# State-space stage: the time steps' sums and rows, and the steps of groups 0 and 1, in later slots

## The chip, the core and the metric
The kernel runs on one core of one Trainium2 chip. The metric is the device time of one execution in microseconds; several executions of the same program give a median. TensorE (PE) multiplies matrices, VectorE (DVE) and ScalarE (ACT) work elementwise, GpSimd (POOL) computes the low parts of the weights, and SyncE (SP) issues the weight transfers.

## What is computed
Two blocks of a network run on 512 tokens of width 1024: a first block with a state-space branch, a dilated attention branch and a feed-forward part, then a second block of two layers with a gated delta rule and sparse attention. The change touches the state-space branch of the first block alone. What it computes, cut to its core:

```python
z, xbc, dt_raw, q, k, v, g_ssd, g_attn = jnp.split(rms_norm(x, norm1_g) @ w_in, IN_SPLITS, axis=-1)
xbc = silu(causal_dwconv(xbc, conv_w, conv_b))          # 8 groups of 4 heads: X (2 tiles), B, C
dt = softplus(dt_raw + dt_bias); A = -exp(a_log)
a_cs = cumsum(dt * A)                                   # per head, in chunks of 128 time steps
Ldec = exp(where(causal, a_cs[l] - a_cs[s], -inf))
y_diag = einsum(C, B, Ldec, X * dt)
states = einsum(B, exp(a_cs[-1] - a_cs), X * dt)        # carried from chunk to chunk
y_off = einsum(C, previous state, exp(a_cs))
y = (y_diag + y_off + d_skip * xs) * silu(z)
```

## The kernel before
All products run in fp32r with every operand split in a high and a low part. Weights come as a stream of units of 2048 columns (1 MB each): SyncE transfers a unit to `w_raw`, ScalarE writes its high part `w_hi` (L358, `split_unit`), GpSimd subtracts for the low part `w_lo` (L350, four instructions), and TensorE multiplies. A unit holds two half units. One half unit is one call of `gemm` (L369): 16 matmuls with `w_hi` (L379, L380), then 8 with `w_lo` (L385), all into one PSUM bank `g`. This is called a product below. The first product on a unit waits for its `w_hi`, and its last 8 matmuls for its `w_lo`.

The state-space stage goes through slots, numbered (g, n) with n from 0 to 3 and written out by `ssd_slots` (L756). Each slot has one product. In slots (0,0) to (7,3) its result is convolved over time and goes through a silu: for each, ScalarE taps the bank to `s_cv` (L889), VectorE adds three shifted taps (L962, `convolved`), ScalarE writes the silu to `s_xbc` (L904). Slot (g,n) is tile n of group g: 0 and 1 are X, 2 is B, 3 is C. TensorE has made the products of g = 0 before the loop. From slot (8,0) on the products are those of z.

Behind the product of each slot stand the steps of a group x, one each slot, with four slots for each group, from (x+1, 0) on:
- step 0, the turning (`turn`): TensorE transposes X and B (L784, L788) to `p` banks 0 to 2 and multiplies B with C into `p[3]` (L791, the score products); ScalarE copies B (L899); VectorE makes X times the time steps (L975) and masks the score products (L979);
- step 1, the decays (`decays`, L799): four matmuls spread rows of `s_rows` over the partitions, ScalarE takes their exponentials (`s_eb`, L916), VectorE makes two segments (L991, L994), ScalarE their exponentials (L878, heads 0 and 1);
- step 2, the states (`states`, L808): three matmuls, VectorE the other two segments, ScalarE their exponentials (heads 2 and 3), VectorE two scores (L998);
- step 3: VectorE the other two scores, and the recurrence of the states to `s_st` (L1003 to L1011);
- a slot later TensorE makes the group's output (L823, L825), which VectorE reads (L953).

Ahead of all groups stand the time steps. VectorE makes `s_a` in slot (0,1) (L702, with `s_pick` as its last write, L706). TensorE sums it in `pe_dt_sums` (L639, L640), VectorE copies the sums and makes the decay's argument (`dve_dt_decay`, L713 to L718), TensorE turns the copy in rows (`pe_dt_rows`, L727), ScalarE copies the rows (`act_dt_rows`, L734), VectorE corrects a part of them (`dve_dt_rows`, L740). All four stand before or in slot (1,0).

The order on each engine is written out by hand and every engine works strictly in its order; semaphores count up and waits are for the next count.

Of the kernel before, what the change touches and what calls it, by code (L numbers as in the profile page):

```python
# [20 lines left out]
P = 128  # L21
# [701 lines left out]
def pe_dt_rows(K, pe, pos):  # L723
    pe.wait_ge(K.sem("dt_a"), pos.next("dt_a"))
    pe.wait_ge(K.sem("g_free3"), pos.next("g_free3"))
    for c in range(NB):
        last = K.nc.tensor.matmul(K.g[3][:, c * P:c * P + P], K.s_acs4[:, c], K.mask("ident"),  # L727
                                  start=True, stop=True)
    last.then_inc(K.sem("turned"), 1)


def act_dt_rows(K, act, pos):
    act.wait_ge(K.sem("turned"), pos.next("turned"))
    act.activation(K.s_rows[:], K.g[3][:], ACT.Copy).then_inc(K.sem("exp_out"), 1)  # L734


def dve_dt_rows(K, dve, pos):
    dve.wait_ge(K.sem("exp_out"), pos.next("exp_out", 2))
    r = slice(32, 64)
    K.nc.vector.tensor_tensor(K.s_rows[r], K.g[3][r], K.s_rows[r].bitcast(F32), ALU.subtract).then_inc(pos.own, pos.tick())  # L740
    dve.wait_ge(pos.own, pos.ticks())
    dve.sem_inc(K.sem("g_free3"), 1)
# [13 lines left out]
def ssd_slots():  # L756

    slots, turn = [], 0
    for i in range(4 * GROUPS + 16):
        x, step = i // 4 - 1, i % 4  # L760
        core = (x, step) if 0 <= x < GROUPS else None
        out = x - 1 if step == 0 and 1 <= x <= GROUPS else None
        z = i - 4 * GROUPS if i >= 4 * GROUPS else None
        ring = {}
        for use, there in (("half", True), ("y", out is not None), ("sum", z is not None and z % 2 == 0 and z > 0)):
            if there and i == 3:
                ring[use] = 3
            elif there:
                ring[use] = turn % 3
                turn += 1  # L770
        slots.append((i // 4, step, z, core, out, ring))
    return slots


def pe_ssd(K, pe, pos):
# [3 lines left out]
    def turn(x):  # L779
# [9 lines left out]
        last.then_inc(K.sem("turned"), 1)  # L789
        for c in range(NB):  # L790
            last = t.matmul(K.p[3][:, c * P:c * P + P], xbc[:, 2, c * P:c * P + P], xbc[:, 3, c * P:c * P + P],  # L791
                            start=True, stop=True)
# [9 lines left out]
    def states(x):  # L802
        if x:
            pe.wait_ge(K.sem("y_read"), pos.next("y_read", 2))
        pe.wait_ge(K.sem("x2"), pos.next("x2"))
# [28 lines left out]
    for g, n, z, core, out, ring in ssd_slots():  # L834
# [4 lines left out]
        if (g, n) == (1, 0):  # L839
            pe_dt_sums(K, pe, pos)  # L840
            pe_dt_rows(K, pe, pos)
# [29 lines left out]
def act_ssd(K, act, pos):  # L871
# [10 lines left out]
    for g, n, z, core, out, ring in ssd_slots():  # L882
# [4 lines left out]
        b, step = ring["half"], None if core is None else core[1]  # L887
        if z is None:
            act.activation(K.s_cv[:, n % 2], K.g[b][:], ACT.Identity, scale=K.col("conv_w", g * 16 + n * 4 + 3),  # L889
                           bias=K.col("conv_b", g * 4 + n)).then_inc(K.sem("tap"), 1)  # L890
        else:
            if z == 0:
                act.wait_ge(K.sem("y_read"), pos.next("y_read", 14))
            act.activation(K.z_s[:, z % 2], K.g[b][:], ACT.Silu).then_inc(K.sem("z_s"), 1)
        if n % 2 and (g, n) != (0, 1):
            split_unit(K, act, pos, n // 2)
        if step == 0:
# [4 lines left out]
        if z is None:  # L902
            act.wait_ge(K.sem("conv"), pos.next("conv"))
            act.activation(K.s_xbc[:, g % 2, n], K.s_cv[:, n % 2], ACT.Silu).then_inc(K.sem("xbc"), 1)  # L904
# [15 lines left out]
        if (g, n) == (0, 3):  # L920
            act_dt_decay(K, act, pos)
            act_dt_rows(K, act, pos)
# [24 lines left out]
def dve_ssd(K, dve, pos):  # L947
# [71 lines left out]
    for g, n, z, core, out, ring in ssd_slots():  # L1019
# [5 lines left out]
        x, step = core if core is not None else (None, None)  # L1025
        if out is not None:
# [12 lines left out]
        else:  # L1039
# [3 lines left out]
            dve.sem_inc(K.sem(f"g_free{b}"), 1)  # L1043
        if step == 0:
# [4 lines left out]
        elif step == 2:  # L1049
            scores(0)  # L1050
            scores(1)
        if (g, n) == (0, 1):
            dve_dt(K, dve, pos)
        if (g, n) == (0, 3):
            dve_dt_decay(K, dve, pos)
            dve_dt_rows(K, dve, pos)
# [1906 lines left out]
```

## Time and profile before
| | |
|---|---|
| median of 3 runs | 3738.72 us (3729.16 to 3741.48) |
| profiled execution, its own time | 3724.99 us |
| its span | 3723.2 us, granted TensorE clock 0.986 of full |
| PE busy | 3611.1 us, 97% |
| DVE busy | 1820.8 us, 49% |
| ACT busy | 1410.3 us, 38% |
| POOL busy | 1406.1 us, 38% |

Times in the rows are microseconds from the start of the span. A row of the timeline has the start, the duration of the merged instructions, the engine, the line of the kernel, the operation, the tiles it writes and reads, their shapes, the count, and in square brackets the idle time of the engine ahead of it and what ended it.

### The profile page before, as it was taken

What the parts mean: (1) busy time and instruction counts of PE and PEld (TensorE: products, weight loads), DVE (VectorE), ACT (ScalarE), POOL (GpSimd) and SP (SyncE); (2) the same over time, 40 slices, a digit from 0 to 9 for tenths busy, and PEclk for the clock granted to TensorE, in tenths of its full rate; (3) what the DMA queues carried; (4) which work ended last, traced back from release to release, by engine and by line L of the source; (5) the groups of instructions that cost most, each with busy time, mean ns of one, the idle gap of its engine ahead of it and who ended that gap; (6) DMA issues with size and microseconds to landing.
All of it is one profiled execution on the core that took longest, in us unless ns stands there. A gap on an engine that the chain in (4) does not pass through costs nothing.

```text
span 3723.2 us, 48288 instructions
## 1 busy us (share of the span) xinstructions
PE 3611.1 (97%) x18696; PEld 2996.3 (80%) x18696; DVE 1820.8 (49%) x3291; ACT 1410.3 (38%) x2039; POOL 1406.1 (38%) x1092
## 2 busy tenths in 40 slices
PE   6999999999999999999999999999999999899998
PEld 5887888777788888888778988888888877888887
DVE  5887516654788664456475451113112467542111
ACT  5666424544322232223345442223222435543222
POOL 2333443223444444434311044445445421115444
PEclk9999999999999999999999999999999999999999
DMA  3121222111355655555310022223222310012222
GB/s 119 70 76 60 93 101 71 56 68 57 113 191 190 208 191 195 185 200 178 102 35 35 1 102 102 84 94 117 102 81 101 125 46 35 24 46 91 102 85 108
DMA packets 67325, 375.99 MB, mean 101 GB/s; under 512 B 7856, under 2 KB 8368, under 8 KB 39344
## 3 DMA queue, kind: packets, MB, share of 16 engines
q1 hardware_dynamic: 44192, 286.11, 21.5%
q10 hardware_dynamic: 22928, 86.99, 7.0%
q8 instruction: 147, 2.41, 0.3%
q14 instruction: 58, 0.48, 0.0%
HBM read 370.97 MB, written 2.10 MB: 100 GB/s over the span
## 4 chain that ended last, share of the span: by engine, by line
PE 57%; issue 24%; POOL 12%; DVE 4%; ACT 1%; POOLq 0%; DVEq 0%; ACTq 0%
PE g L379 13%; PE g L380 12%; PE g L385 12%; POOL w_lo L350 12%; PE g L364 3%; PE g L365 2%; PE g L366 2%; PE p L1899 1%; PE p L2075 1%; PE g L1878 1%; PE p L1889 1%; PE p L2081 1%; PE g L624 1%; PE g L620 1%; PE g L619 1%
## 5 line engine op out<-in xcount | busy, mean ns | idle before, releaser
L350 POOL TENSOR_TENSOR w_lo<-w_raw,w_hi 128x512 fp32r<-128x512 f32 (+1 forms) x1088 | 1405.9, 1324 | 2310.0 <-ACT w_hi L358 2310.0
L379 PE MATMUL g<-h_lo,w_hi 128*128 128x512 f32 x2400 | 949.3, 396 | 3.7 <-ACT w_hi L358 1.6
L380 PE MATMUL g<-h_hi,w_hi 128*128 128x512 f32 x2400 | 935.5, 390 | 0.0
L358 ACT ACTIVATE w_hi<-w_raw 128x2048 fp32r<-128x2048 f32 (+1 forms) x292 | 515.8, 1766 | 941.4 <-PE g L385 867.1
L385 PE MATMUL g<-h_hi,w_lo 128*128 128x512 f32 x2400 | 592.8, 389 | 1.2 <-POOL w_lo L350 1.2
L379 PEld LDWEIGHTS g<-h_lo,w_hi 128*128 128x128 f32 x2400 | 450.7, 188 | 106.4 <-issue 8.6
L380 PEld LDWEIGHTS g<-h_hi,w_hi 128*128 128x128 f32 x2400 | 450.7, 188 | 95.3 <-issue 3.1
L385 PEld LDWEIGHTS g<-h_hi,w_lo 128*128 128x128 f32 x2400 | 450.4, 188 | 95.1 <-POOL w_lo L350 1.6
L379 PE MATMUL g<-act_lo,w_hi 128*128 128x512 f32 x880 | 346.1, 393 | 0.0
L380 PE MATMUL g<-act_hi,w_hi 128*128 128x512 f32 x880 | 343.1, 390 | 0.0
L1650 DVE TENSOR_TENSOR p<-f_acc,g 128x512 f32<-128x512 f32 x84 | 58.5, 696 | 564.4 <-PE g L385 563.2
L1498 DVE SCALAR_TENSOR_TENSOR p<-ada_w,csilu,p 128x256 f32<-128x256 f32 x432 | 211.6, 490 | 52.4 <-DMA ada_w<-in_ada 29.6
L385 PE MATMUL g<-act_hi,w_lo 128*128 128x512 f32 x880 | 212.5, 389 | 0.0
L379 PEld LDWEIGHTS g<-act_lo,w_hi 128*128 128x128 f32 x880 | 165.3, 188 | 34.1
L385 PEld LDWEIGHTS g<-act_hi,w_lo 128*128 128x128 f32 x880 | 165.2, 188 | 34.3
L380 PEld LDWEIGHTS g<-act_hi,w_hi 128*128 128x128 f32 x880 | 165.3, 188 | 33.9
L364 PE MATMUL g<-h_hi,w_lo 128*128 128x512 f32 x416 | 179.5, 431 | 0.9 <-POOL w_lo L350 0.9
L1462 DVE SCALAR_TENSOR_TENSOR x<-g,mods,x 128x512 f32<-128x512 f32 x48 | 35.9, 749 | 277.9 <-PE g L385 267.3
L365 PE MATMUL g<-h_lo,w_hi 128*128 128x512 f32 x416 | 167.7, 403 | 0.0
L366 PE MATMUL g<-h_hi,w_hi 128*128 128x512 f32 x416 | 167.2, 402 | 0.0
L1580 ACT ACTIVATE f_acc<-g 128x512 f32<-128x512 f32 x84 | 50.2, 598 | 258.1 <-PE g L385 249.9
L1629 DVE TENSOR_TENSOR act_lo<-p,act_hi 128x512 fp32r<-128x512 f32 x110 | 76.1, 692 | 119.3 <-ACT act_hi L1561 108.1
(484 smaller groups left out, 5175.6 us busy)
## 6 DMA issues: line engine op xcount, KB each, us to landing
w_raw<-in_stream SPq DMA_DIRECT2D x212, 1024.0 KB, 4.8
ada_w<-in_ada ACTq DMA_DIRECT2D x144, 512.0 KB, 4.1
w_raw<-in_stream SPq DMA_DIRECT2D x80, 704.0 KB, 4.1
ada_w<-in_stream ACTq DMA_DIRECT2D x8, 512.0 KB, 4.4
n_w<-in_w ACTq DMA_DIRECT2D x4, 1024.0 KB, 10.1
x<-in_x SPq DMA_DIRECT2D x4, 512.0 KB, 9.7
b_w<-in_stream ACTq DMA_DIRECT2D x2, 1024.0 KB, 4.8
out_x<-x SPq DMA_DIRECT2D x4, 512.0 KB, 2.6
```

The source lines that it names most:

```text
L350: last = K.nc.gpsimd.tensor_tensor(K.w_lo[:, s, c], K.w_raw[:, s, c], K.w_hi[:, s, c].bitcast(F32), ALU.subtract)
L358: act.activation(K.w_hi[:, s, 0:width], K.w_raw[:, s, 0:width], ACT.Copy).then_inc(K.sem("w_hi"), 1)
L364: nc.tensor.matmul(out, w_lo, h_hi, start=start, stop=False)
L365: nc.tensor.matmul(out, w_hi, h_lo, start=False, stop=False)
L366: return nc.tensor.matmul(out, w_hi, h_hi, start=False, stop=stop)
L379: t.matmul(K.g[b][:], K.w_hi[:, s, w], lo[:, k, :], start=starts and i == 0, stop=False)
L380: t.matmul(K.g[b][:], K.w_hi[:, s, w], hi[:, k, :], start=False, stop=False)
L385: last = t.matmul(K.g[b][:], K.w_lo[:, s, w], hi[:, k, :], start=False, stop=ends and i == len(ks) - 1)
L1498: v.scalar_tensor_tensor(out, w[:, i * 256:i * 256 + 256], scalar(i), acc, ALU.mult, ALU.add).then_inc(pos.own, pos.tick())
L1580: act.activation(K.f_acc[:, s], K.g[2 * s][:], ACT.Silu).then_inc(K.sem("f_s"), 1)
L1629: v.tensor_tensor(K.act_lo[:, u], K.p[1 if conv else u % 2][:], K.act_hi[:, u].bitcast(F32), ALU.subtract).then_inc(K.sem("act_lo"), 1)
L1650: v.tensor_tensor(K.p[s][:], K.f_acc[:, s], K.g[2 * s + 1][:], ALU.mult).then_inc(K.sem("f_u"), 1)
```

## The change
- The sums of the time steps (`pe_dt_sums`) stand behind the product of slot (1,1), not (1,0); the rows (`pe_dt_rows`) behind that of (1,2), and they use the bank `p[3]` and not `g[3]`. The bank is handed on by a semaphore of its own, `dt_rows`, for which the score products of group 0 wait.
- VectorE's decay steps stand ahead of the convolution of slot (0,3), not behind it. `act_dt_rows` stands in slot (1,2) behind the tap, `dve_dt_rows` in slot (1,2) behind the convolution.
- Group 0 begins in slot (1,2) and not (1,0), group 1 in slot (2,1) and not (2,0). Both have three slots: VectorE makes all four scores and the recurrence in the slot of step 2. The outputs of groups 0 and 1 stand in slots (2,1) and (3,0); before, in (2,0) and (3,0). From group 2 on nothing is moved.
- Since group 0 still reads its half of `s_xbc` in slot (2,1), ScalarE writes the silus of (2,0) and (2,1) together there, after waiting for VectorE to have read the output, and waits ahead of the tap of (2,2) for the first of them.

```diff
--- before.py
+++ after.py
@@ -722,23 +722,23 @@

 def pe_dt_rows(K, pe, pos):
     pe.wait_ge(K.sem("dt_a"), pos.next("dt_a"))
-    pe.wait_ge(K.sem("g_free3"), pos.next("g_free3"))
     for c in range(NB):
-        last = K.nc.tensor.matmul(K.g[3][:, c * P:c * P + P], K.s_acs4[:, c], K.mask("ident"),
+        last = K.nc.tensor.matmul(K.p[3][:, c * P:c * P + P], K.s_acs4[:, c], K.mask("ident"),
                                   start=True, stop=True)
     last.then_inc(K.sem("turned"), 1)


 def act_dt_rows(K, act, pos):
     act.wait_ge(K.sem("turned"), pos.next("turned"))
-    act.activation(K.s_rows[:], K.g[3][:], ACT.Copy).then_inc(K.sem("exp_out"), 1)
+    act.activation(K.s_rows[:], K.p[3][:], ACT.Copy).then_inc(K.sem("exp_out"), 1)


 def dve_dt_rows(K, dve, pos):
     dve.wait_ge(K.sem("exp_out"), pos.next("exp_out", 2))
     r = slice(32, 64)
-    K.nc.vector.tensor_tensor(K.s_rows[r], K.g[3][r], K.s_rows[r].bitcast(F32), ALU.subtract).then_inc(pos.own, pos.tick())
-    dve.wait_ge(pos.own, pos.ticks())
+    K.nc.vector.tensor_tensor(K.s_rows[r], K.p[3][r], K.s_rows[r].bitcast(F32), ALU.subtract
+                              ).then_inc(K.sem("dt_rows"), 1)
+    dve.wait_ge(K.sem("dt_rows"), pos.next("dt_rows"))
     dve.sem_inc(K.sem("g_free3"), 1)


@@ -756,10 +756,12 @@
 def ssd_slots():

     slots, turn = [], 0
+    begins = [6, 9] + [4 * x + 4 for x in range(2, GROUPS)]
+    cores = {at + step: (x, step) for x, at in enumerate(begins) for step in range(4 if x > 1 else 3)}
+    outs = {9 if x == 0 else 4 * x + 8: x for x in range(GROUPS)}
     for i in range(4 * GROUPS + 16):
-        x, step = i // 4 - 1, i % 4
-        core = (x, step) if 0 <= x < GROUPS else None
-        out = x - 1 if step == 0 and 1 <= x <= GROUPS else None
+        step = i % 4
+        core, out = cores.get(i), outs.get(i)
         z = i - 4 * GROUPS if i >= 4 * GROUPS else None
         ring = {}
         for use, there in (("half", True), ("y", out is not None), ("sum", z is not None and z % 2 == 0 and z > 0)):
@@ -787,6 +789,8 @@
         for c in range(NB):
             last = t.transpose(K.p[2][:, c * P:c * P + P], xbc[:, 2, c * P:c * P + P], ident)
         last.then_inc(K.sem("turned"), 1)
+        if x == 0:
+            pe.wait_ge(K.sem("dt_rows"), pos.next("dt_rows"))
         for c in range(NB):
             last = t.matmul(K.p[3][:, c * P:c * P + P], xbc[:, 2, c * P:c * P + P], xbc[:, 3, c * P:c * P + P],
                             start=True, stop=True)
@@ -802,6 +806,8 @@
     def states(x):
         if x:
             pe.wait_ge(K.sem("y_read"), pos.next("y_read", 2))
+        else:
+            pe.wait_ge(K.sem("g_free3"), pos.next("g_free3"))
         pe.wait_ge(K.sem("x2"), pos.next("x2"))
         pe.wait_ge(K.sem("seg"), pos.next("seg"))
         for c in range(3):
@@ -836,8 +842,9 @@
         if g == 0:
             continue
         gemm(K, pos, s, (ring["half"],), K.h_hi, K.h_lo, c0=n % 2 * P, fresh=n % 2 == 0)
-        if (g, n) == (1, 0):
+        if (g, n) == (1, 1):
             pe_dt_sums(K, pe, pos)
+        if (g, n) == (1, 2):
             pe_dt_rows(K, pe, pos)
         if out is not None:
             output(out, ring["y"])
@@ -885,23 +892,30 @@
         else:
             act.wait_ge(K.sem("part"), pos.next("part"))
         b, step = ring["half"], None if core is None else core[1]
+        if (g, n) == (2, 2):
+            act.wait_ge(K.sem("xbc"), 9)
         if z is None:
             act.activation(K.s_cv[:, n % 2], K.g[b][:], ACT.Identity, scale=K.col("conv_w", g * 16 + n * 4 + 3),
                            bias=K.col("conv_b", g * 4 + n)).then_inc(K.sem("tap"), 1)
         else:
             if z == 0:
-                act.wait_ge(K.sem("y_read"), pos.next("y_read", 14))
+                act.wait_ge(K.sem("y_read"), pos.next("y_read", 12))
             act.activation(K.z_s[:, z % 2], K.g[b][:], ACT.Silu).then_inc(K.sem("z_s"), 1)
         if n % 2 and (g, n) != (0, 1):
             split_unit(K, act, pos, n // 2)
+        if (g, n) == (1, 2):
+            act_dt_rows(K, act, pos)
         if step == 0:
             act.wait_ge(K.sem("turned"), pos.next("turned"))
             act.activation(K.s_btok[:].rearrange("p c n -> p (c n)"), K.p[2][:], ACT.Copy).then_inc(K.sem("turned_out"), 1)
         if step == 2:
             exps(core[0], (2, 3))
         if z is None:
-            act.wait_ge(K.sem("conv"), pos.next("conv"))
-            act.activation(K.s_xbc[:, g % 2, n], K.s_cv[:, n % 2], ACT.Silu).then_inc(K.sem("xbc"), 1)
+            if (g, n) == (2, 1):
+                act.wait_ge(K.sem("y_read"), pos.next("y_read", 2))
+            for m in {(2, 0): (), (2, 1): (0, 1)}.get((g, n), (n,)):
+                act.wait_ge(K.sem("conv"), pos.next("conv"))
+                act.activation(K.s_xbc[:, g % 2, m], K.s_cv[:, m % 2], ACT.Silu).then_inc(K.sem("xbc"), 1)
         elif z % 2 == 0 and z:
             z_deviation(K, act, pos, K.g[ring["sum"]])
         elif z % 2:
@@ -919,7 +933,6 @@
             act_dt(K, act, pos)
         if (g, n) == (0, 3):
             act_dt_decay(K, act, pos)
-            act_dt_rows(K, act, pos)
     pos.skip("y_read", 2)


@@ -1023,6 +1036,8 @@
             pos.skip("part")
         b = ring["half"]
         x, step = core if core is not None else (None, None)
+        if (g, n) == (0, 3):
+            dve_dt_decay(K, dve, pos)
         if out is not None:
             output(out, ring["y"])
         if step == 1:
@@ -1041,6 +1056,8 @@
             v.tensor_tensor(K.y[:, z], K.y[:, z], K.z_s[:, z % 2], ALU.mult).then_inc(K.sem("z_y"), 1)
             dve.wait_ge(K.sem("z_y"), pos.next("z_y"))
             dve.sem_inc(K.sem(f"g_free{b}"), 1)
+        if (g, n) == (1, 2):
+            dve_dt_rows(K, dve, pos)
         if step == 0:
             inputs(x)
         elif step == 1:
@@ -1049,11 +1066,12 @@
         elif step == 2:
             scores(0)
             scores(1)
+            if x < 2:
+                scores(2)
+                scores(3)
+                states(x)
         if (g, n) == (0, 1):
             dve_dt(K, dve, pos)
-        if (g, n) == (0, 3):
-            dve_dt_decay(K, dve, pos)
-            dve_dt_rows(K, dve, pos)
         if z is not None and z > 1:
             if z % 2 == 0:
                 z_normal(K, dve, pos, z // 2 - 1, ring["sum"])
```

TensorE, slots (1,0) and (1,1), behind the 8 matmuls with `w_lo` that end the product of (1,0); L784 to L791 are the turning of group 0. Before:

```order
L385 MATMUL g<-h_hi,w_lo 128x512 x8
L639 MATMUL p<-s_a,masks 128x128
L640 MATMUL p<-s_a,masks 128x128
L727 MATMUL g<-masks,s_acs_93 128x128 x4
L784 MATMUL p<-masks,s_xbc 128x128 x8
L788 MATMUL p<-masks,s_xbc 128x128 x4
L791 MATMUL p<-s_xbc 128x128 x4
L379 MATMUL g<-h_lo,w_hi 128x512
```

With the change, behind the product of slot (1,2); the two sums alone stand one product earlier:

```order
L385 MATMUL g<-h_hi,w_lo 128x512 x8
L726 MATMUL p<-masks,s_acs_93 128x128 x4
L786 MATMUL p<-masks,s_xbc 128x128 x8
L790 MATMUL p<-masks,s_xbc 128x128 x4
L795 MATMUL p<-s_xbc 128x128 x4
L379 MATMUL g<-h_lo,w_hi 128x512
```

Rows and turning have moved two products back.

VectorE, group 0, from the last segment to the output (L953, with the change L966). Before:

```order
L994 TENSOR_TENSOR s_ce<-s_xbc,s_eb 128x512
L962 SCALAR_TENSOR_TENSOR s_cv<-g,cols,s_cv 128x511
L962 SCALAR_TENSOR_TENSOR s_cv<-g,cols,s_cv 128x510
L962 SCALAR_TENSOR_TENSOR s_cv<-g,cols,s_cv 128x509
L998 TENSOR_TENSOR s_m<-s_m,s_cbt 128x512 x4
L1003 COPY s_st<-g 128x256
L1007 TENSOR_TENSOR s_st<-s_st,s_eb 128x256
L1011 TENSOR_TENSOR s_st<-s_st,g 128x256
L1007 TENSOR_TENSOR s_st<-s_st,s_eb 128x256
L1011 TENSOR_TENSOR s_st<-s_st,p 128x256
L962 SCALAR_TENSOR_TENSOR s_cv<-g,cols,s_cv 128x511
```

With the change:

```order
L1007 TENSOR_TENSOR s_ce<-s_xbc,s_eb 128x512
L975 SCALAR_TENSOR_TENSOR s_cv<-g,cols,s_cv 128x511
L975 SCALAR_TENSOR_TENSOR s_cv<-g,cols,s_cv 128x510
L975 SCALAR_TENSOR_TENSOR s_cv<-g,cols,s_cv 128x509
L1011 TENSOR_TENSOR s_m<-s_m,s_cbt 128x512 x4
L1016 COPY s_st<-g 128x256
L1020 TENSOR_TENSOR s_st<-s_st,s_eb 128x256
L1024 TENSOR_TENSOR s_st<-s_st,g 128x256
L1020 TENSOR_TENSOR s_st<-s_st,s_eb 128x256
L1024 TENSOR_TENSOR s_st<-s_st,p 128x256
L966 SCALAR_TENSOR_TENSOR y<-s_xbc,cols,g 128x512 x2
```

Up to the last step of the states the list is the same; behind it the convolution (three instructions) that stood ahead of the output is gone.

ScalarE, group 1, from the exponentials of its decays (L916) to the silu's table load: in the second piece a weight unit (L358) stands between the tap and the second half of the exponentials. Before:

```order
L916 ACTIVATE s_eb<-p 128x512 x4
L878 ACTIVATE s_m<-s_m,s_nacs 128x128 x8
L889 ACTIVATE s_cv<-g,cols 128x512
L878 ACTIVATE s_m<-s_m,s_nacs 128x128 x8
L904 ACT_TABLE_LOAD
```

With the change:

```order
L930 ACTIVATE s_eb<-p 128x512 x4
L885 ACTIVATE s_m<-s_m,s_nacs 128x128 x8
L898 ACTIVATE s_cv<-g,cols 128x512
L358 ACTIVATE w_hi<-w_raw 128x2048
L885 ACTIVATE s_m<-s_m,s_nacs 128x128 x8
L918 ACT_TABLE_LOAD
```

The split has moved ahead of the exponentials of heads 2 and 3.

## Rows read from the trace of the kernel before
**Rows 1.** The page, part 1: busy time, share of the span, instructions.
```profile
PE 3611.1 (97%) x18696; PEld 2996.3 (80%) x18696; DVE 1820.8 (49%) x3291; ACT 1410.3 (38%) x2039; POOL 1406.1 (38%) x1092
```
**Rows 2.** Timeline of PE, 60 to 140 us: start, duration, what.
```profile
67.34 0.77 PE L639 MATMUL p<-s_a,masks 128*128 128x128 f32 x2 [4.97 <-DVE s_pick L706]
...
74.83 2.08 PE L727 MATMUL g<-masks,s_acs 128*128 128x128 f32 x8 [6.30 <-DVE s_acs L718]
...
78.80 1.06 PE L791 MATMUL p<-s_xbc 128*128 128x128 f32 x8
...
79.61 0.47 PE L379 MATMUL g<-h_lo,w_hi 128*128 128x512 f32 x1
...
85.18 1.09 PE L799 MATMUL p<-s_rows,s_pick 128*128 128x512 f32 x4
...
104.54 0.68 PE L823 MATMUL g<-s_m,s_X 128*64 128x128 f32 x8
...
107.77 1.09 PE L784 MATMUL p<-masks,s_xbc 128*128 128x128 f32 x8
...
115.51 1.07 PE L799 MATMUL p<-s_rows,s_pick 128*128 128x512 f32 x4
...
134.87 0.68 PE L823 MATMUL g<-s_m,s_X 128*64 128x128 f32 x8
```
**Rows 3.** Stretches, PE alone: us, length, busy, granted clock, DMA share, GB/s.
```profile
64.00:66.00 2.00, 0.00 (x0) 0.66 0.00 0
...
78.00:80.00 2.00, 2.00 (x17) 0.92 0.57 143
```
**Rows 4.** Timeline of DVE, 67 to 105 us.
```profile
67.11 2.31 DVE L962 SCALAR_TENSOR_TENSOR s_cv<-g,cols,s_cv 128x511 f32<-128x511 f32 x3
...
73.25 0.29 DVE L713 COPY s_acs<-p 128x128 f32<-128x128 f32 x1
...
74.10 0.68 DVE L718 COPY s_acs<-p 128x512 f32<-128x512 f32 x1
...
77.58 0.68 DVE L740 TENSOR_TENSOR s_rows<-g,s_rows 32x512 fp32r<-32x512 f32 x1 [2.80 <-ACT s_rows L734]
...
91.12 0.69 DVE L991 TENSOR_TENSOR s_m<-p,s_acs 128x512 f32<-128x512 f32 x1 [2.61 <-ACT s_eb L916]
...
98.87 2.50 DVE L998 TENSOR_TENSOR s_m<-s_m,s_cbt 128x512 f32<-128x512 f32 x4
...
102.66 1.28 DVE L1007 TENSOR_TENSOR s_st<-s_st,s_eb 128x256 f32<-128x256 f32 x1
...
103.97 0.42 DVE L1011 TENSOR_TENSOR s_st<-s_st,p 128x256 f32<-128x256 f32 x1
```
**Rows 5.** Timeline of ACT, 69 to 76 us.
```profile
69.99 0.76 ACT L889 ACTIVATE s_cv<-g,cols 128x512 f32<-128x512 f32 x1
70.65 1.90 ACT L358 ACTIVATE w_hi<-w_raw 128x2048 fp32r<-128x2048 f32 x1
73.14 0.63 ACT L904 ACTIVATE s_xbc<-s_cv 128x512 f32<-128x512 f32 x1 [0.58 <-DVE s_cv L962]
73.78 1.28 ACT L663 ACT_TABLE_LOAD   x1
75.08 0.31 ACT L663 ACTIVATE s_dec<-s_dec 128x128 f32<-128x128 f32 x1
```
**Rows 6.** Timeline of POOL, 72 to 78 us.
```profile
72.63 4.95 POOL L350 TENSOR_TENSOR w_lo<-w_raw,w_hi 128x512 fp32r<-128x512 f32 x4 [18.93 <-ACT w_hi L358]
```
**Rows 7.** Timeline of PE, DVE and POOL late in the stage, 318 to 332 us.
```profile
326.72 1.15 PE L823 MATMUL g<-s_m,s_X 128*64 128x128 f32 x8 [8.73 <-DVE s_st L1011]
...
331.98 1.98 PE L856 MATMUL g<-z_q,masks 128*128 128x512 f32 x4
...
320.39 3.41 DVE L998 TENSOR_TENSOR s_m<-s_m,s_cbt 128x512 f32<-128x512 f32 x2
...
318.31 6.62 POOL L350 TENSOR_TENSOR w_lo<-w_raw,w_hi 128x512 fp32r<-128x512 f32 x4 [12.63 <-ACT w_hi L358]
```

## Prediction
> **What bounds the kernel now.** I read the page first: TensorE is busy for 97% of the span [rows 1], so this change, which moves work inside one stage, can only matter where TensorE stands still there or will come to do so. The next view is the timeline of TensorE around the first state-space groups. It stands still twice: 4.97 us before the sums of the time steps and 6.30 us before their rows [rows 2]. Behind the first pause the granted clock falls from 2.4 to 1.2 GHz (0.66 in 64 to 66 us, a mixture of the two levels) and is whole again only within 78 to 80 us (0.92) [rows 3], so the work between the pauses and just behind them runs at half speed. That is the prize: 11.3 us of idle time and about 2 us of slow clock.
>
> The third view is the same timeline further on, since the change also squeezes groups 0 and 1. From the first matmul of a group's decays to the first of its output, TensorE takes 85.18 to 104.54 us for group 0, and 115.51 to 134.87 us for group 1: 19.36 us both times [rows 2]. In that stretch it runs three products (a product is the 24 matmuls of one half unit, 79.61 to 85.18, 5.57 us [rows 2]) and the states. The fourth view, VectorE and ScalarE over the same 19.36 us, says who sets that length: VectorE's last step of the states starts at 103.97 and takes 0.42, and the output starts 0.15 us behind it [rows 2, 4]. So TensorE now has exactly enough products to cover the other two engines, and none to spare.
>
> **Part 1, sums and rows of the time steps.** The product of slot (1,1) now stands in the 4.97 us pause. It starts at 62.4 (67.34 less 4.97 [rows 2]) and ends near 68.0, and the sums follow at once, since what they need has come at 67.34. The 6.30 us pause is filled only partly. The product of slot (1,2) is the first on another weight unit, whose high part ScalarE splits from 70.65 for 1.90 us [rows 5], so it can't start before 72.6. TensorE pauses from about 68.5 to 72.6. Its low part is ready when GpSimd ends, 72.63 + 4.95 = 77.6 [rows 6], so this product ends near 79.4; the rows and the first turning then end by 81.4 (from 74.83 to 78.80 they take 4.0 at the low clock [rows 2], so about 2.0 at the high one). Nothing is lost by any of this yet.
>
> The score products of group 0 are the first that wait for `dt_rows`. In VectorE's queue that step now stands behind the convolution of slot (1,2), and this ends a ladder in which the two engines take turns. VectorE has convolved slot (0,2) at 67.11 + 2.31 = 69.4 [rows 4]. The decay steps follow, 1.5 us (from 73.25 to 0.68 past 74.10 [rows 4]), to 71.0; the convolution of (0,3), 2.31, to 73.3; ScalarE's silu 0.63, table load 1.28 and exponential 0.31 [rows 5], to 75.6. Each slot now costs 0.76 + 2.31 + 0.63 = 3.7 us [rows 4, 5]: two slots bring 83.0, the first tap and the convolution of (1,2) 86.1, and the row step 0.68 [rows 4] 86.8. TensorE had reached this point by 81.4, so it waits about 5 us: a new stall in place of the old one. Before, the row step stood ahead of that ladder, at 77.58 [rows 4].
>
> From there: score products 0.81 (78.80 to 79.61), the product of (1,3) 5.57 [rows 2], and about 2.0 for a clock that falls in a pause of this size. For that 2.0 the nearest row is the stall of 8.73 us late in the stage: the output behind it takes 326.72 to 331.98, 5.26 us, against 104.54 to 107.77, 3.23 us [rows 2, 7]. The decays of group 0 start at 86.8 + 0.8 + 5.6 + 2.0 = 95.2, where before they started at 85.18. They then have two products more behind them, so against the old order TensorE is 85.18 + 2 x 5.57 - 95.2 = 1.1 us ahead: of the 13.4 us hardly anything is left.
>
> **Part 2, three slots for each of the first two groups.** Decays, states and output of group 0 now stand in slots (1,3), (2,0) and (2,1): two products between decays and output, not three. VectorE's work in between is the same list (four segments, one convolution, four scores, the states), because the second convolution was behind the states before and is behind them now. Nothing in that list but its head waits for TensorE. So the output starts 19.36 us after the decays, and TensorE, with one product less to do, stands still for 5.57 us. This comes once in each group.
>
> Group 0: output at 95.2 + 19.4 = 114.6. From there the output, the turning of group 1 and a product take 104.54 to 115.51, 10.97 us [rows 2], plus 2.0 for the clock: decays of group 1 at 127.5.
>
> Group 1: its second exponentials now fall into slot (2,3), in which ScalarE first splits a weight unit (1.90 [rows 5]); before, that slot of the group had no split. The exponentials still come in time, but GpSimd's four subtractions now run beside VectorE's scores. With GpSimd beside them two scores took 3.41 us [rows 7], where four took 2.50 [rows 4], so 2.2 more for two. I take 2.2 for the four; 0 if GpSimd comes late, 4.3 if all four are caught. The trace shows it also at 102.66, where a step of the states takes 1.28 [rows 4]. The Trainium skill, page "SBUF — State Buffer", section "Who interferes with whom", says that a VectorE instruction with two inputs in SBUF and a GpSimd instruction that reads SBUF exclude each other for a whole instruction. The scores are of that kind and the trace agrees (1.7 us for one of 0.62); by the rule alone the cost would be at most four GpSimd instructions, near my upper end.
>
> Output of group 1: 127.5 + 19.4 + 2.2 = 149.1, and 2.0 for the clock: 151.1. From that point both orders have the same work behind and ahead of them; before, it was reached at 134.87 [rows 2].
>
> **Sum: +16.3 us**, call it 16. In it: -1.1 up to the decays of group 0, two stalls of 5.6, two low clocks of 2.0, and GpSimd 2.2. Against the profiled execution (span 3723.2, its time 3725.0) this makes 3741. That execution is faster than two of the three runs shown; on their median, 3738.7, it makes **3755 us** (+0.43%). The bounds: if the clock never falls in the three new stalls, 6 us less; if GpSimd meets nothing, 2.2 less; so +8. With all four scores caught and another step of the states in each group (1.28 for about 0.4), +20. Later stages follow TensorE and are only shifted: the weight transfers are issued as GpSimd frees a unit, which follows the products. The deferred silus of slot (2,0) are hidden: ScalarE has the whole product of (2,2) for them.
>
> **The rivals.**
> *A small loss.* Same stalls, but the clock keeps its level and GpSimd's work lands between VectorE's steps: +8 to +11, 3747 to 3750. For it: a stall of 5 us is shorter than the one of 8.7 I took the price from. Against it: the clock fell in the pause of 4.97 us already [rows 2, 3].
> *The stalls don't come, not slower.* One mechanism: the distance from decays to output is elastic, and shrinks to the 13.8 us of TensorE's own work (19.36 - 5.57). Then output 1 starts at 86.8 + 0.8 + 5.6 + 13.8 + 11.0 + 13.8 = 131.8, 3 us early, 3736; if the row step comes without a wait too, some 8 us early, 3730; and if the product of (1,2) finds its unit ready the whole 13.4 is gained, 3725. It decides at a distance of 15.3 us, where the output would start at 134.87. For it: VectorE idles 2.6 us ahead of the first segment, waiting for ScalarE [rows 4]. Against it: both groups show the same 19.36, and behind that first segment VectorE works without a pause to the end of the states.
> *A larger loss.* The stalls repeat in group 2, or the clock stays low through a whole product: over +20, above 3759. Against it: group 2 has its four slots again.
>
> **How the numbers follow.** The smallest change that a measurement of this kernel tells from none is about 0.3%, 11.2 us. The forecast, between +11.2 and +20, has 0.60 and lies wholly on the slower side; a small loss 0.22, within 0.3%; the elastic distance 0.13, of which 0.08 faster by over 0.3% and 0.05 within it; a larger loss 0.05. That gives faster 0.08, same 0.27, slower 0.65. The range leaves out the elastic distance and most of the larger loss, takes in +8 on a run a few microseconds below the median and +20 with as much above: 3740 to 3763.
>
> **What would show it.** In the new profile: the waits for `s_pick` and for the decay copy are gone from TensorE; its score products wait some 5 us for VectorE's row step; the output of groups 0 and 1 waits some 5.5 us and up to 8 us for the last step of the states; decays to output is again about 19.4 us for group 0, and 20 to 22 for group 1; the granted clock shows three low spells between 82 and 155 us; output 1 starts near 149. The prediction is wrong if the output waits stay under 2 us, if the row step ends before 82 us, or if the start of output 1 lies before 140.

## The result and the profile after

| | before | with the change |
|---|---|---|
| median | 3729.19 us (13 runs, 3723.83 to 3741.48) | 3744.76 us (13 runs, 3738.76 to 3755.09) |
| ratio | | 1.0041, 95% interval 1.0029 to 1.0052 |
| profiled execution, span | 3723.2 us | 3751.6 us |
| mean granted clock | 0.986 | 0.982 |
| PE busy | 3611.1 us | 3626.5 us |

The change makes the kernel 15.6 us slower, 0.41%, with an interval of 0.29 to 0.52%. The profiled execution of the changed kernel (3753.4 us by its own time) is one of its slower ones, so the spans differ by 28.4 us, more than the medians do. Where the change itself stands in the trace is read from the first and last start of two groups of matmuls behind the stage: first the products on the finished state-space output (`y_hi`), then those on the activations of the feed-forward parts. Before:

```profile
L380 PE MATMUL g<-y_hi,w_hi x128: 389/389/389, 448.2 to 531.1; 128*128 128x512 f32 x128
...
L380 PE MATMUL g<-act_hi,w_hi x880: 389/389/397, 1229.8 to 3705.1; 128*128 128x512 f32 x176
```

With the change:

```profile
L380 PE MATMUL g<-y_hi,w_hi x128: 389/389/389, 464.2 to 547.1; 128*128 128x512 f32 x128
...
L380 PE MATMUL g<-act_hi,w_hi x880: 387/389/398, 1246.0 to 3734.3; 128*128 128x512 f32 x176
```

At 448 us the delay is 16.0, at 1230 it is 16.2: nothing is given back and nothing added over these stages. The 12 us more by the end of this one execution (28.4 less 16.2) arise behind 1246 us, where no instruction has moved; they are not in the medians.

TensorE's waits between 50 and 160 us, with the change:

```profile
PE g L829 <- DVE s_st L1024: 13.9, 2, 7.6
PE g L379 <- ACT w_hi L358: 4.3, 1, 4.3
PE p L795 <- DVE s_rows L739: 3.6, 1, 3.6
```

Both old pauses (4.97 and 6.30 us [rows 2]) are gone; in their place stand four: for the weight unit, for the row step, and for the last step of the states ahead of each of the first two outputs. The timeline of TensorE, answering to [rows 2] (L803 are the decays, L829 the output, L786 the turning of the next group):

```profile
72.38 0.79 PE L379 MATMUL g<-h_lo,w_hi 128*128 128x512 f32 x1 [4.34 <-ACT w_hi L358]
...
80.48 1.05 PE L726 MATMUL p<-masks,s_acs 128*128 128x128 f32 x8
...
86.47 1.16 PE L795 MATMUL p<-s_xbc 128*128 128x128 f32 x8 [3.63 <-DVE s_rows L739]
...
92.96 1.09 PE L803 MATMUL p<-s_rows,s_pick 128*128 128x512 f32 x4
...
113.00 1.15 PE L829 MATMUL g<-s_m,s_X 128*64 128x128 f32 x8 [6.24 <-DVE s_st L1024]
...
119.00 1.10 PE L786 MATMUL p<-masks,s_xbc 128*128 128x128 f32 x8
...
126.75 1.07 PE L803 MATMUL p<-s_rows,s_pick 128*128 128x512 f32 x4
...
148.15 1.15 PE L829 MATMUL g<-s_m,s_X 128*64 128x128 f32 x8 [7.61 <-DVE s_st L1024]
...
161.41 1.09 PE L803 MATMUL p<-s_rows,s_pick 128*128 128x512 f32 x4
```

Read it in the steps of the sum. Decays to output (92.96 to 113.00, 126.75 to 148.15) is 20.04 us in group 0 and 21.40 in group 1, where it was 19.36 in both. The output itself takes 6.0 us (113.00 to 119.00) and not 3.23, since it starts at the low clock. The decays of group 2 start at 161.41. In the kernel before they start at 145.85, one period of 30.34 us behind those of group 1 [rows 2]:

```profile
145.85 1.09 PE L799 MATMUL p<-s_rows,s_pick 128*128 128x512 f32 x4
```

The difference is 15.6 us, which is that of the medians.

VectorE over the same time:

```profile
85.73 0.68 DVE L739 TENSOR_TENSOR s_rows<-p,s_rows 32x512 fp32r<-32x512 f32 x1
...
106.64 2.50 DVE L1011 TENSOR_TENSOR s_m<-s_m,s_cbt 128x512 f32<-128x512 f32 x4
...
109.51 1.48 DVE L1020 TENSOR_TENSOR s_st<-s_st,s_eb 128x256 f32<-128x256 f32 x1
...
139.95 5.89 DVE L1011 TENSOR_TENSOR s_m<-s_m,s_cbt 128x512 f32<-128x512 f32 x4
```

and GpSimd beside the last of these rows:

```profile
138.99 6.30 POOL L350 TENSOR_TENSOR w_lo<-w_raw,w_hi 128x512 fp32r<-128x512 f32 x4 [24.24 <-ACT w_hi L358]
```

The row step ends at 86.4. The four scores of group 1 take 5.89 us instead of 2.50 [rows 4], with GpSimd's four subtractions beside them, which themselves take 6.30 instead of 4.95 [rows 6].

The granted clock (us, length, PE busy, clock, DMA share, GB/s):

```profile
70.00:72.00 2.00, 0.00 (x0) 0.74 0.00 0
...
76.00:78.00 2.00, 2.00 (x7) 0.56 0.00 0
...
84.00:86.00 2.00, 0.00 (x0) 1.00 0.00 0
...
112.00:114.00 2.00, 1.00 (x10) 0.50 0.03 8
...
146.00:148.00 2.00, 0.00 (x0) 0.50 0.68 197
```

There are three low spells. Each begins in a pause of TensorE (of 4.34, 6.24 and 7.61 us) and reaches into the work behind it. In the pause of 3.63 us, in which TensorE stands from 82.8 to 86.5, the clock stays at 2.4 GHz.

### The profile page after: what moved, and what is told of

Same layout as the page of the kernel before. It is cut to its first block, busy times and chain, and to the rows that moved or that the text cites. A ratio compares the mean times of both kernels' runs of the same rounds, so it can differ in the third digit from the quotient of the medians.

```text
span 3751.6 us, 48289 instructions
## 1 busy us (share of the span) xinstructions
PE 3626.5 (97%) x18696; PEld 3008.2 (80%) x18696; DVE 1823.9 (49%) x3291; ACT 1409.5 (38%) x2039; POOL 1405.6 (37%) x1092
## 4 chain that ended last, share of the span: by engine, by line
PE 47%; issue 31%; POOL 16%; DVE 5%; ACT 1%; POOLq 0%; DVEq 0%; ACTq 0%
POOL w_lo L350 16%; PE g L379 9%; PE g L380 9%; PE g L385 9%; PE g L364 2%; PE g L366 2%; PE g L365 2%; PE p L1917 2%; PE p L2093 1%; PE g L1896 1%; PE p L1907 1%; PE p L2099 1%; PE p L1929 1%; PE g L620 0%; PE g L624 0%
## 5 line engine op out<-in xcount | busy, mean ns | idle before, releaser
L358 ACT ACTIVATE w_hi<-w_raw 128x2048 fp32r<-128x2048 f32 (+1 forms) x292 | 515.6, 1766 | 937.6 <-PE g L385 863.3
```

What stands on the lines that cost most here:

```text
L358: act.activation(K.w_hi[:, s, 0:width], K.w_raw[:, s, 0:width], ACT.Copy).then_inc(K.sem("w_hi"), 1)
```

## The experiments

The landmark is the start of the decays of group 2, behind which all these kernels but the last have the same work left. It is measured from the start of the write of `s_pick`, which does not depend on the edits: 78.8 us in the kernel before, 94.6 with the change. Landmarks and distances are each read from the one profiled execution of a kernel, and a fall of the clock that comes in one execution and not in another moves them by some 1.6 us, as `split_behind` shows. `split_behind`, `rows_early` and `conv_behind` were executed only once, so they have no median to compare.

### The stalls with TensorE kept at work

```diff
     def output(x, b):
-        pe.wait_ge(K.sem("mce"), pos.next("mce", 4))
+        if x < 2:
+            pe.wait_ge(K.sem("mce"), pos.next("mce", 1))
+            for i in range((16, 24)[x]):
+                t.matmul(K.p[3][:], K.mask_r[:, 0], K.h_hi[:, i % 8], start=True, stop=True)
+        pe.wait_ge(K.sem("mce"), pos.next("mce", 3 if x < 2 else 4))
```

> The changed kernel, with TensorE given idle work in the two stalls ahead of the outputs of groups 0 and 1: once the first score of the group is made, 16 and 24 matmuls whose result nobody reads. Theory (the stalls are set by VectorE and ScalarE, and the low clock behind them is a cost of its own): output 0 still starts near 113 us and output 1 at 21.4 us behind its decays, but the granted clock stays at full, so output 0 to the decays of group 1 takes 11.0 us and not 13.75, and the decays of group 2 start some 5 us earlier than 161.4, at 156 to 157. Rival (the clock costs nothing, since the other engines set the pace there as well): the decays of group 2 start at 161 as in the changed kernel.

Measured: the matmuls nobody reads, and the output behind them.

```profile
107.55 3.93 PE L823 MATMUL p<-h_hi,mask_r 128*128 128x512 f32 x16 [0.65 <-DVE s_m L1015]
...
113.18 0.68 PE L833 MATMUL g<-s_m,s_X 128*64 128x128 f32 x8 [1.70 <-DVE s_st L1028]
...
116.41 1.09 PE L786 MATMUL p<-masks,s_xbc 128*128 128x128 f32 x8
...
124.14 1.07 PE L803 MATMUL p<-s_rows,s_pick 128*128 128x512 f32 x4
...
145.63 0.68 PE L833 MATMUL g<-s_m,s_X 128*64 128x128 f32 x8 [1.59 <-DVE s_st L1028]
```

Output 0 starts when it did, 20.05 us behind its decays, though TensorE now works almost up to it: the other engines set that distance. The output takes 3.23 us again, and output 0 to the decays of group 1 takes 10.96 and not 13.75. The landmark is at 89.6, 5.0 us earlier; the ratio to the kernel before is 1.0029 (1.0015 to 1.0044). So of the 15.6 us, 5.0 are the clock behind the two stalls.

### The split behind the exponentials

```diff
-        if n % 2 and (g, n) != (0, 1):
+        if n % 2 and (g, n) not in ((0, 1), (2, 3)):
             split_unit(K, act, pos, n // 2)
...
         if step == 2:
             exps(core[0], (2, 3))
+        if (g, n) == (2, 3):
+            split_unit(K, act, pos, n // 2)
```

> The changed kernel, with ScalarE splitting the weight unit of slot (2,3) behind the second exponentials of group 1 and not ahead of them. Theory (GpSimd's four subtractions beside VectorE's scores made the four scores take 5.89 us and not 2.50): the scores take about 2.5 us, one or two steps of the states may take up to 1.3 us more each instead, and decays to output of group 1 is 19.4 to 21 us, not 21.40. The decays of group 2 start 1 to 2 us earlier than 161.4. Rival (the scores are slow for want of the exponentials): they stay at 5 to 6 us.

```profile
140.52 3.56 DVE L1013 TENSOR_TENSOR s_m<-s_m,s_cbt 128x512 f32<-128x512 f32 x4
...
144.46 1.03 DVE L1022 TENSOR_TENSOR s_st<-s_st,s_eb 128x256 f32<-128x256 f32 x1
...
145.98 0.92 DVE L1022 TENSOR_TENSOR s_st<-s_st,s_eb 128x256 f32<-128x256 f32 x1
```

The scores take 3.56 us, not 5.89 (expected were 2.5), though their exponentials now come earlier, not later: the rival falls. GpSimd begins at 141.90, 1.4 us into the scores, and the part of them that is slow follows it. 2.3 us are won there, and two steps of the states lose 1.1 together (1.03 and 0.92 for 0.43 each). Decays to output of group 1 is 20.17 us instead of 21.40. The landmark gains only 0.3 us, at 94.3: in this execution the clock fell in the pause ahead of the score products, and the product of slot (1,3) took longer (decays of group 0 at 27.8 from `s_pick`, not 26.2), which took back 1.6. By that distance the edit is worth 1.2 us; that the landmark gained less than the 1 to 2 us expected is the clock's doing.

### The rows behind the sums

```diff
         if (g, n) == (1, 1):
             pe_dt_sums(K, pe, pos)
-        if (g, n) == (1, 2):
             pe_dt_rows(K, pe, pos)
...
-        if (g, n) == (1, 2):
-            act_dt_rows(K, act, pos)
...
             act_dt_decay(K, act, pos)
+            act_dt_rows(K, act, pos)
...
-        if (g, n) == (1, 2):
+        if (g, n) == (1, 0):
             dve_dt_rows(K, dve, pos)
```

> The changed kernel, with the rows of the time steps right behind the sums in slot (1,1), ScalarE's copy at the end of slot (0,3) and VectorE's row step behind the convolution of slot (1,0). Theory (the score products of group 0 wait 3.63 us for a row step that stands behind a ladder of convolutions): this wait is gone, the rows fit in the pause ahead of the product of slot (1,2), and the decays of group 0 start some 3.5 us earlier, near 89.5 and not 92.96; everything behind moves with them, output 1 to near 144.5. Rival (the distance from decays to output is elastic and takes up the gain): output 1 stays at 148.

```profile
71.69 1.16 PE L726 MATMUL p<-masks,s_acs 128*128 128x128 f32 x8 [2.71 <-DVE s_acs L718]
73.32 0.80 PE L379 MATMUL g<-h_lo,w_hi 128*128 128x512 f32 x1 [0.48 <-ACT w_hi L358]
...
89.10 1.19 PE L803 MATMUL p<-s_rows,s_pick 128*128 128x512 f32 x4 [0.82 <-DVE s_cbt L990]
...
107.84 1.15 PE L829 MATMUL g<-s_m,s_X 128*64 128x128 f32 x8 [4.84 <-DVE s_st L1022]
...
141.57 1.15 PE L829 MATMUL g<-s_m,s_X 128*64 128x128 f32 x8 [7.59 <-DVE s_st L1022]
```

The wait for the row step is gone, and the rows fit in the pause for the weight unit. The decays of group 0 start 21.4 us behind `s_pick` (89.10 less 67.73) instead of 26.2: 4.8 us. 3.6 of them are the wait, less 0.8 for a new one for VectorE's inputs; 0.9 come since the rows' matmuls stand in the pause, and 1.0 since the product of (1,2) is done sooner (the turning starts 12.7 us behind `s_pick`, against 80.48 less 66.78, 13.7, for the rows ahead of it). The landmark is at 86.4, 8.3 us earlier. The other 3.5 are not that wait. 1.3 of them lie in the distance to output 0, which is 18.7 and not 20.0, as GpSimd's subtractions now meet fewer of VectorE's steps (the first of the states takes 0.42 us and not 1.48). 2.1 lie behind the two outputs, where the low clock costs 1.4 and 1.6 us and not 2.8 and 2.3. Whether a second execution would give these 3.5 again is not shown. The elastic rival falls: the gain grows on its way, it is not taken up.

### One group with three slots in the kernel before

```diff
-        out = x - 1 if step == 0 and 1 <= x <= GROUPS else None
+        out = 0 if i == 7 else x - 1 if step == 0 and 2 <= x <= GROUPS else None
...
-        elif step == 3:
+        elif step == 3 and x:
             scores(2)
             scores(3)
             states(x)
...
             scores(0)
             scores(1)
+            if x == 0:
+                scores(2)
+                scores(3)
+                states(x)
```

> The kernel before with one edit: group 0 has three slots, its scores and states in slot (1,2) and its output in slot (1,3), one slot earlier. Theory (decays to output takes 19.4 us whatever TensorE has to do): output 0 still starts at 104.5 us, now with one product less behind it, so TensorE stands still for about 5.5 us ahead of it and runs slowly for some 2 us behind it; the decays of group 2, 145.8 before, come 7 to 8.5 us later. Rival (the distance is elastic and shrinks to TensorE's own 13.9 us): output 0 starts near 99, and nothing behind moves by more than 1 us.

```profile
86.27 1.09 PE L799 MATMUL p<-s_rows,s_pick 128*128 128x512 f32 x4
...
105.59 1.15 PE L823 MATMUL g<-s_m,s_X 128*64 128x128 f32 x8 [5.53 <-DVE s_st L1011]
...
154.87 1.09 PE L799 MATMUL p<-s_rows,s_pick 128*128 128x512 f32 x4
```

This is the cleanest test, as nothing of the time steps is moved. Decays to output takes 19.32 us, as ever, and TensorE stands still for 5.53 us: the length of one product. The landmark is 87.2, 8.4 us later than before: 5.6 for the product, 2.4 for the slow clock behind the stall (18.95 us from output 0 to the decays of group 1, less 10.97 and one product), and 0.4 that arose ahead of the decays of group 0 (18.6 us from `s_pick`, not 18.2). The ratio is 1.0021 (1.0007 to 1.0036), some 8 us: half of what the whole change costs comes with one group that has lost a slot.

### The convolutions behind the states

```diff
         if z is None:
-            convolved(g, n, b)
+            if (g, n) not in ((2, 0), (2, 3)):
+                convolved(g, n, b)
...
                 states(x)
+            if (g, n) in ((2, 0), (2, 3)):
+                convolved(g, n, b)
```

> The changed kernel, with VectorE's convolutions of slots (2,0) and (2,3) behind the states of groups 0 and 1 and no longer ahead of their scores. Theory (behind its first segment VectorE's list sets the distance from decays to output): decays to output falls by one convolution, 2.3 to 2.5 us, in each of the two groups: from 20.04 to about 17.7 and from 21.40 to about 19; the decays of group 2 start 4 to 5 us earlier than 161.4. Rival (something else than VectorE's list sets it, ScalarE's exponentials or TensorE's states): the distances change by less than 1 us.

The decays and outputs of groups 0 and 1:

```profile
94.28 1.09 PE L803 MATMUL p<-s_rows,s_pick 128*128 128x512 f32 x4
...
110.30 0.68 PE L829 MATMUL g<-s_m,s_X 128*64 128x128 f32 x8 [2.24 <-DVE s_st L1024]
...
122.92 1.07 PE L803 MATMUL p<-s_rows,s_pick 128*128 128x512 f32 x4
...
142.09 1.15 PE L829 MATMUL g<-s_m,s_X 128*64 128x128 f32 x8 [5.39 <-DVE s_st L1024]
```

The distances fall to 16.02 and 19.17, by 4.0 and 2.2 us. The theory said one convolution each, 2.3. Group 0 gains 1.6 more because its states now end before GpSimd begins: both their steps take 0.43 us, not 1.48 and 0.92. In group 1 the 2.2 agree only by luck. VectorE, two of its four scores:

```profile
136.28 0.73 DVE L1011 TENSOR_TENSOR s_m<-s_m,s_cbt 128x512 f32<-128x512 f32 x1 [1.32 <-ACT s_m L885]
137.45 1.23 DVE L1011 TENSOR_TENSOR s_m<-s_m,s_cbt 128x512 f32<-128x512 f32 x1 [0.44 <-ACT s_m L885]
```

VectorE now waits 1.8 us for ScalarE's second exponentials, which stand behind the weight split there, so in this group the rival holds for a part. This loss was made up, as the scores, which now begin ahead of GpSimd, themselves take 3.3 us and not 5.89, against 1.1 more for the states. The landmark is at 88.2, 6.4 us earlier; the clock behind the outputs gave 1.8 of it, and took 1.6 ahead of the decays of group 0.

### Three edits together

> The changed kernel with three edits together: rows behind the sums, the two convolutions behind the states, the split of slot (2,3) behind the exponentials. Theory (three causes in a row on one chain, so their costs add): from the start of s_pick to the decays of group 2, 94.6 us in the changed kernel and 78.8 before, it takes 94.6 - 8.3 - 4.7 - 1 = 81 us (by the runs of the first two edits 8.3 and about 1, by estimate 4.7), still 1 to 3 us more than before; the time is within 0.15% of before. Rival (the causes cover each other): 84 us or more.

This is the changed kernel with the rows behind the sums, the convolutions behind the states, and the split behind the exponentials, by the three diffs above. The landmark is at 80.4, expected 81; the ratio to the kernel before is 1.0000 (0.9987 to 1.0013). The waits ahead of the two outputs are 1.96 and 2.94 us. The causes lie on one chain and their costs nearly add: the single gains were 8.3, 6.4 and 0.3 us, together 15.0, and the three edits together win 14.2. Mended, the change is worth nothing: two groups still have a slot too few, and these two waits with the low clock behind them (1.7 and 2.9 us) make 9.5 us. The first of them:

```profile
104.02 0.68 PE L829 MATMUL g<-s_m,s_X 128*64 128x128 f32 x8 [1.96 <-DVE s_st L1024]
```

and the clock behind it:

```profile
104.00:106.00 2.00, 1.98 (x30) 0.81 0.04 8
```

### TensorE one product ahead, all groups with four slots

The core of the edit to the kernel before, on TensorE; beside it the bank `p[3]` with the semaphore `dt_rows` as in the change, ScalarE's copy of the rows behind the split of slot (0,3), and VectorE's decay steps ahead of the convolution of (0,3) with the row step behind it.

```diff
-        if (g, n) == (1, 0):
+        if (g, n) == (1, 1):
             pe_dt_sums(K, pe, pos)
             pe_dt_rows(K, pe, pos)
...
+        if g == 1:
+            core = (0, n - 1) if n else None
         if core is not None and core[1] < 3:
             (turn, decays, states)[core[1]](core[0])
```

> The kernel before, every group with its four slots and its output where it was. TensorE makes the product of slot (1,1) ahead of the sums, rows and turning of group 0, and that of (1,2) ahead of its decays; VectorE makes its decay steps ahead of the convolution of (0,3), ScalarE copies the rows right behind the split. Theory (the idle time before the rows can be filled if nothing is put behind the ladder and no group loses a slot): the row step ends near 74 us, the turning near 76, and ScalarE and VectorE, which now set the pace, bring output 0 near 98.5 to 101 and not 104.5, after a stall of TensorE of 2 to 5 us; the decays of group 2 start 3 to 6 us earlier than 145.8, and the time is 3 to 6 us lower, 0.1 to 0.15%. Rival (each product moved forward is paid for again by a stall of its own length): the decays of group 2 at 145 to 147, the time as before.

The row step on VectorE:

```profile
73.03 0.68 DVE L739 TENSOR_TENSOR s_rows<-p,s_rows 32x512 fp32r<-32x512 f32 x1 [0.57 <-ACT s_rows L733]
```

and TensorE:

```profile
82.90 1.09 PE L801 MATMUL p<-s_rows,s_pick 128*128 128x512 f32 x4
...
98.43 0.68 PE L827 MATMUL g<-s_m,s_X 128*64 128x128 f32 x8 [2.23 <-DVE s_st L1018]
```

and the clock behind its start:

```profile
98.00:100.00 2.00, 1.57 (x29) 1.00 0.00 0
```

Of the 11.3 us of pauses 5.4 stay gone: the landmark is at 73.4 against 78.8, within what was expected. The ratio is 0.9990 (0.9978 to 1.0001), a median 3.8 us lower but not clear of no change by itself. Decays to output of group 0 is 15.5 us here and not 19.4. So the 19.36 us are no fixed time of the other engines behind the decays. Before, ScalarE's tap of slot (1,1), which with a convolution and a silu stands ahead of the exponentials, waits for the product that ends as the decays start. Here that product was done one product earlier, and the exponentials start 2.8 us behind the decays instead of 5.3. In the three-slot groups of the changed kernel the decays again follow directly on the product that the tap waits for, and the exponentials start 5.3 us behind them.

### The same for the late stall

```diff
             scores(2)
             scores(3)
             states(x)
+            if z == 3:
+                z_normal(K, dve, pos, 0, z_bank)
...
-            if z % 2 == 0:
+            if z == 2:
+                z_bank = ring["sum"]
+            elif z % 2 == 0:
                 z_normal(K, dve, pos, z // 2 - 1, ring["sum"])
```

> The kernel of turn_one_later with one more edit of the same kind, late in the stage: VectorE makes the last two scores and the states of group 7 ahead of the normalisation of the first two z tiles, not behind it. Theory (output 7 waits 8.7 us only because the list on VectorE ahead of the states holds 5.8 us of normalisation, with 3.75 us of waiting for ScalarE ahead of it, and the clock falls behind that wait): the wait ahead of output 7 falls to under 2 us, the output takes 3.2 and not 5.3 us; if the normalisation becomes late for nobody, the stage is 8 to 10 us shorter than that of turn_one_later, 13 to 15 us shorter than before, and the time 0.3 to 0.4% below before. Rival (the stall moves: the normalisation's bank and the squares behind it come late and TensorE waits there for as long): under 3 us gained over turn_one_later.

TensorE's waits, 60 to 400 us:

```profile
PE g L379 <- DVEq L1054: 2.7, 1, 2.7
...
PE g L862 <- DVEq L1054: 2.4, 1, 2.4
PE g L827 <- DVE s_st L1018: 2.4, 2, 2.3
```

The wait of 8.7 us ahead of output 7 [rows 7] is gone, the output takes 3 us again, but two waits of 2.4 and 2.7 us on VectorE's next steps have come behind it, so theory and rival each hold for a part. Behind the second of them the matmuls take 0.63 us instead of 0.39, so the clock has fallen there too. The products on `y_hi` start at 438.2 us; in `turn_one_later` at 442.7, before at 448.2. That is 4.5 us gained over `turn_one_later`, where 8 to 10 were expected. The ratio to the kernel before is 0.9979 (0.9967 to 0.9992): this version is faster than the kernel before by 0.2%, which is clear of no change but less than the 0.3 to 0.4% expected.

## Why the prediction was right

The forecast was slower, by 16 us; measured are 15.6. The mechanism held. That the sum of 16.3 came within 0.7 us is luck in part, since its terms missed by up to 2.2 us and in both directions. The absolute figure, 3755, is 10 us too high, since the median of three runs that it was put on, 3738.7, lies above the 3729.2 of thirteen.

*The time steps.* The row step was to end at 86.8 us and ended at 86.4: the ladder of taps, convolutions and silus was read correctly, and `rows_early` shows that it is the cause. TensorE came to it at 82.8 and not 81.4, since the clock fell already in the pause for the weight unit (0.74 in 70 to 72 us), which I had not counted. It cost nothing there, as TensorE had to wait for VectorE anyway. The wait was 3.6 us, not 5.

*The clock behind that wait.* Here a term was wrong: I took 2.0 us for a fall in a pause of 3.6 to 5 us and it did not come, so the decays of group 0 started at 92.96 and not 95.2. In two of the other runs, `split_behind` and `conv_behind`, it did come, after the same pause, and cost 1.6 us. So of the three low spells that were to show between 82 and 155 us there are two; the third of the profile lies earlier, behind the pause for the weight unit.

*The three-slot groups.* The forecast was one product, 5.57 us, of stall in each. `old_three_slots` shows it alone: 5.53 us and an unchanged 19.3 from decays to output. In the changed kernel the stalls are 6.24 and 7.61, because VectorE's list is longer by what GpSimd adds: 0.7 us in group 0, for which I had only a place in the upper bound, and 2.0 in group 1, where the forecast was 2.2. The four scores alone lost 3.4, near my upper end of 4.3; the steps of the states behind them, slow in the other groups, were free again and gave 0.9 of it back, and 0.5 came back ahead of them, where one instruction had taken 1.17 us and now took 0.68. The rule of the Trainium skill (page "SBUF — State Buffer", section "Who interferes with whom") fits: four instructions of 1.24 us could have cost 5.0 at most, and `split_behind` moves the loss with GpSimd.

*The clock behind the stalls.* Forecast 2.0 each; measured, from each output to the next decays, 2.8 behind output 0 (13.75 less 10.97) and 2.3 behind output 1 (13.26 less 10.97). `stall_filled` gives both back, 5.0 us.

*The rivals.* The elastic distance, in a group that gives up a slot, is refuted by `old_three_slots` and by `rows_early`. The 15.5 us of `turn_one_later` are another case, as there one more product stands between the product that the tap waits for and the decays. The small loss and the larger one did not come. The errors went both ways: 2.2 less at the first clock term, 1.1 more at the later two, 0.5 more for GpSimd.

## What to carry to other kernels

When steps of a pipeline are moved to fill a pause, compare each distance between two of TensorE's steps with the time that the other engines need in between. Where the one exactly covers the other, as with the 19.36 us here, each product taken out of it comes back as a stall of its own length, and in the changed kernel the clock added nearly half as much again. Look also at where the other engines' chain begins: it began here at the end of a product and not at the decays, and having that product done earlier shortened the distance to 15.5 us. Moving the filling work ahead of the waiting step, and the waited-for step ahead of its ladder, won 5 us in the trace where moving the steps back lost 16. An engine's order matters at both ends: what is put behind a ladder waits for all of it.

## What the runs showed of the hardware

The low clock behind the waits of 5.5, 6.2 and 7.6 us in `old_three_slots` and in the changed kernel cost 2.4, 2.8 and 2.3 us more, and in `stall_filled`, where TensorE had work in the pause, it did not come, though nobody reads the result. The length of the pause by itself decides neither whether the clock falls nor what that costs:

- Ahead of the score products of group 0 the clock stayed up behind 3.47 and 3.63 us and fell behind 3.68 and 3.75.
- Ahead of output 0 it fell behind 1.96 us in `three_mended` and 2.24 in `conv_behind`, at a cost of 1.7 us each, and stayed up behind 2.23 in `turn_one_later`.
- Ahead of output 1 it cost 2.9 us behind 2.94 in `three_mended`, and 1.6 behind 7.59 in `rows_early`, where the clock had fallen 3.6 us before TensorE went on.

What decides it these runs do not show. The fall ahead of the score products, in `conv_behind`:

```profile
86.00:88.00 2.00, 1.77 (x11) 0.87 0.20 41
88.00:90.00 2.00, 2.00 (x7) 0.50 0.96 406
```

Two engines that hinder each other lose on both sides: the four scores took 5.89 for 2.50 us, and GpSimd's four subtractions 6.30 for 4.95.
